# Three PSUM banks in turn for the down products of the looped rounds

## What is computed

```python
def swiglu(h, w_gu, w_down):
    gt, up = jnp.split(h @ w_gu, 2, axis=-1)
    return (jax.nn.silu(gt) * up) @ w_down

def short_conv_mixer(h, w_in, w_conv, w_out):
    bg, cg, xv = jnp.split(h @ w_in, 3, axis=-1)
    return (bg * dwconv(cg * xv, w_conv, SC_PAD)) @ w_out

def reference(...):
    h, hc = x, ctx
    for l in range(DEPTH):                      # DEPTH = 2
        sh1, sc1, g1, sh2, sc2, g2 = adaln(c, mod_w[l], mod_b[l])
        n_lat = modulate(rmsnorm(h, norm1_g[l]), sh1, sc1)
        if l % 2 == 0:
            y, yc = hybrid_mixer(n_lat, n_ctx, ...)
        else:
            y = short_conv_mixer(n_lat, o_w_in[o], o_conv_w[o], o_w_out[o])
        h = h + g1 * y
        h = h + g2 * swiglu(modulate(rmsnorm(h, norm2_g[l]), sh2, sc2), ffn_w_gu[l], ffn_w_down[l])
    return rmsnorm(h, final_g)
```

## Time and profile before

| | |
|---|---|
| median of 3 runs | 2563.57 us (2562.7 to 2565.39) |
| the profiled execution | 2565.16 us, its span 2563.0 us |
| TensorE busy | 2459.5 us, 96% of the span |
| VectorE busy | 1128.1 us, 44% |
| TensorE waiting for sumsq (normalisations) | 27.8 us, 5 times |
| TensorE waiting for an update of h | 21.7 us, 37 times |
| mean granted clock of TensorE | 0.989 |

### The profile page before, as it was taken

How to read it: one execution, slowest core, us unless ns; L and a number is a source line. 1 busy time by engine, 2 the same in 40 slices (tenths; PEclk the granted TensorE clock), 3 DMA queues, 4 the chain that set the end, 5 groups by cost and what they waited for, 6 DMA issues and landing times.

```text
span 2563.0 us, 29648 instructions
## 1 busy us (share of the span) xinstructions
PE 2459.5 (96%) x11210; PEld 1996.6 (78%) x11210; DVE 1128.1 (44%) x1460; ACT 524.7 (20%) x805; POOL 1067.1 (42%) x511
## 2 busy tenths in 40 slices
PE   7899999989899999999999899999799999999999
PEld 3677877768788888888888688887688888888887
DVE  4666648755843444422223634245622222222224
ACT  3344437751200000000001200002200000000003
POOL 2143336899533444333444234342533333333440
PEclk9999999999999999999999899999899999999999
DMA  9543366433233332311111011111111111111111
GB/s 284 149 134 128 128 174 135 89 97 107 91 115 115 112 100 91 105 50 49 49 49 50 17 50 50 41 50 40 50 50 42 48 49 41 49 49 49 49 33 66
DMA packets 223198, 206.55 MB, mean 81 GB/s; under 512 B 40119, under 2 KB 193427, under 8 KB 222611
## 3 DMA queue, kind: packets, MB, share of 16 engines
q1 hardware_dynamic: 216643, 186.64, 25.1%
q10 hardware_dynamic: 5904, 16.78, 1.7%
q0 software_dynamic: 576, 2.10, 0.2%
HBM read 185.20 MB, written 20.28 MB: 80 GB/s over the span
## 4 chain that ended last, share of the span: by engine, by line
PE 85%; DVE 6%; POOL 3%; issue 3%; ACT 2%; DMA 1%; DVEq 0%; POOLq 0%; SPq 0%; ACTq 0%
PE bank L727 27%; PE bank L729 26%; PE bank L728 26%; DVE h L1365 1%; PE bank L850 1%; DVE probs L1568 1%; DVE sumsq L1321 1%; PE bank L808 1%; POOL k_lo L628 1%; PE bank L759 1%; PE bank L893 1%; DVE act_lo L1348 1%; DMA mod_ring<-in_mod_w 1%; DVE hid_f L1608 1%; ACT probs L1213 1%
## 5 line engine op out<-in xcount | busy, mean ns | idle before, releaser
L574 POOL TENSOR_TENSOR w_hi<-raw,ones 128x1024 fp32r<-128x1024 f32 x200 | 392.3, 1961 | 1240.0 <-PE bank L729 1191.6
L727 PE MATMUL bank<-act_hi,w_hi 128*128 128x512 f32 x2176 | 855.5, 393 | 13.4 <-DVE act_lo L1348 4.5
L728 PE MATMUL bank<-act_hi,w_lo 128*128 128x512 f32 x2176 | 851.7, 391 | 0.0
L729 PE MATMUL bank<-act_lo,w_hi 128*128 128x512 f32 x2176 | 851.6, 391 | 0.0
L577 POOL TENSOR_TENSOR w_lo<-raw,w_hi 128x1024 fp32r<-128x1024 f32 x200 | 509.9, 2550 | 15.7
L727 PEld LDWEIGHTS bank<-act_hi,w_hi 128*128 128x128 f32 x2176 | 411.3, 189 | 103.6 <-issue 7.6
L729 PEld LDWEIGHTS bank<-act_lo,w_hi 128*128 128x128 f32 x2176 | 411.1, 189 | 86.1
L728 PEld LDWEIGHTS bank<-act_hi,w_lo 128*128 128x128 f32 x2176 | 411.5, 189 | 84.5
L1365 DVE SCALAR_TENSOR_TENSOR h<-bank,mods,h 128x512 f32<-128x512 f32 x432 | 320.6, 748 | 244.5 <-PE bank L729 242.4
L1608 DVE TENSOR_TENSOR hid_f<-silu_g,bank 128x512 f32<-128x512 f32 x88 | 60.6, 689 | 706.9 <-PE bank L729 705.6
L727 PE MATMUL bank<-hid_hi,w_hi 128*128 128x512 f32 x704 | 281.2, 399 | 15.8 <-DVE h L1365 15.8
(11 more groups left out here) (187 smaller groups left out, 2329.8 us busy)
## 6 DMA issues: line engine op xcount, KB each, us to landing
raw<-in_ffn_w_gu SPq DMA_DIRECT2D x88, 512.0 KB, 3.9
mod_in_f<-in_mod_w SPq DMA_DIRECT2D x48, 512.0 KB, 4.7
raw<-in_ffn_w_down SPq DMA_DIRECT2D x44, 512.0 KB, 3.6
mod_in_p<-in_mod_w SPq DMA_DIRECT2D x32, 512.0 KB, 6.7
raw<-in_o_w_in SPq DMA_DIRECT2D x24, 512.0 KB, 3.7
raw<-in_e_w_in SPq DMA_DIRECT2D x20, 512.0 KB, 4.9
mod_ring<-in_mod_w SPq DMA_DIRECT2D x16, 512.0 KB, 5.0
raw<-in_e_w_out SPq DMA_DIRECT2D x16, 512.0 KB, 3.9
```

The costliest lines, as they stand in the source:

```text
L574: nc.gpsimd.tensor_tensor(w_hi, raw[:, parity, :], ones[:, 0:1].to_broadcast([P, UNIT]), ALU.mult).then_inc(s_hi, 1)
L727: pe.matmul(dst, w_hi, x_hi, start=first, stop=False)
L728: pe.matmul(dst, w_lo, x_hi, start=False, stop=False)
L729: return pe.matmul(dst, w_hi, x_lo, start=False, stop=last)
```

## The change

`out_groups` and `update` get a number of banks, `turn`: 3 where the round does not feed a normalisation, 2 where it does. Group idx writes bank 4 + idx % turn, so banks 4, 5 and 6 in the looped rounds. Groups below `turn` have no wait any more, but group 0, which waits until all updates of the rounds before are done; group idx from `turn` on waits for update idx - turn.

```diff
+                turn = 3 if norm is None else 2
                 for idx in range(16):
                     half, m = divmod(idx, FT)
-                    pe.wait_ge(s_hup, n0 + idx + 1)
-                    group(half, m, bank[:, 4 + m % 2, :]).then_inc(s_out, 1)
+                    if idx == 0 or idx >= turn:
+                        pe.wait_ge(s_hup, n0 + max(idx - turn, 0) + (3 if idx else 2))
+                    group(half, m, bank[:, 4 + idx % turn, :]).then_inc(s_out, 1)
...
-            def update(n0, idx, gate):
+            def update(n0, idx, gate, turn=2):
...
-                V.scalar_tensor_tensor(out=dst, in0=bank[:, 4 + m % 2, :], scalar=mods[:, gate, m:m + 1], in1=dst,
+                V.scalar_tensor_tensor(out=dst, in0=bank[:, 4 + idx % turn, :], scalar=mods[:, gate, m:m + 1], in1=dst,
...
-                        update(16 * i + OUT_F[layer], idx, MODS * layer + G2)
+                        update(16 * i + OUT_F[layer], idx, MODS * layer + G2, 3)
...
-                    update(16 * i + OUT_F[0], idx, G2)
+                    update(16 * i + OUT_F[0], idx, G2, 3)
...
-                    update(16 * i + OUT_S, idx, MODS + G1)
+                    update(16 * i + OUT_S, idx, MODS + G1, 3)
```

## The result

| | before | after |
|---|---|---|
| median, 4 runs each | 2564.48 us (2562.7 to 2567.2) | 2540.02 us (2538.85 to 2541.62) |
| the profiled execution | 2565.16 us, span 2563.0 | 2539.45 us, span 2537.3 |
| TensorE busy | 2459.5 us, 96% | 2451.8 us, 97% |

What follows compares the result with a forecast made beforehand. TensorE's matmuls plus its holes were taken to bound the kernel. Savings of 10.9 + 10.4 + 2.1 = 23.4 us made 2540.2 us against a median of 2563.57, range 2535 to 2547.

Steps and rivals of the forecast that it cites:

- The sum: All looped rounds: 10.9 plain, 10.4 modulation and 2.1 short-convolution save 23.4 us, giving 2540.2 us.
- The bound: TensorE's matmuls and holes set the time; 29 of 37 waits for h, 13.3 us, lie in looped rounds.
- The plain rounds: Rounds 6 to 9 of layer 0, 0 to 9 of layer 1: group 2's hole goes, 14 x 0.78 = 10.9 us.
- The slack of group 3: Plain rounds, three banks: update 0 is over 0.7 us before group 3 would start.
- The modulation rounds: Six rounds adding a modulation row: holes at groups 2, 4, 7, 10 go, 6 x (1.86 - 0.12) = 10.4 us.
- The term for group 5: Modulation rounds: with 0.13 us of slack behind update 2, group 5 costs 0 to 0.25 us; half was charged.
- The short-convolution rounds: Three looped short-convolution rounds lose a hole of 0.71 us each, 2.1 us.
- The clock: Behind the normalisations the 1.2 GHz level may fall on other matmuls: 3 us either way.
- The wait did not move on to group 5: Rival, modulation rounds: group 5 waits 0.58 us as group 4 did, 2543.0 us; chance 0.05.
- The spacing inside the products: Rival, down products: the new bank order slows steps from 0.227 to 0.233 us, 2551.7 us; chance 0.03.
- something else holds group 2: Rival: something the trace hides behind this wait holds group 2 as long, so no gain, 2563.6 us; chance 0.03.
- The slower rival: TensorE drops to 1.2 GHz, one 1.4 us piece in each of 23 changed rounds, 2572 us; chance 0.02.

Runs made afterwards that it cites:

- the copies: A 128 x 256 VectorE copy added ahead of update 0 in the 14 plain rounds of the changed kernel: within SBUF 2566.92 us, from bank 7 2538.93 us.
- the pair of copies: A 128 x 256 copy out of bank 7 ahead of update 0 in plain rounds: kernel before, two banks, 2569.23 us; changed kernel, three banks, 2538.93 us.
- the run with the SBUF copy and two banks: Kernel before plus a 128 x 256 copy within SBUF ahead of update 0 in the 14 plain rounds: 2615.15 us, ratio 1.0205.
- the last rounds: Changed kernel plus a third bank in the last feed-forward round of layer 0 and the last short-convolution round: 2541.41 us, ratio 0.9911.
- a moved instruction: Kernel before, update 0 moved ahead of the last hid_lo or z_lo: all looped rounds 2557.88 us; 14 plain rounds alone 2565.73 us (2557.27 to 2582.29).

## Why the prediction was right

**The number.** The sum was 23.4 us and the medians say 24.5; the periods say 24.7. That 2540.2 and 2540.02 lie 0.2 us apart is in part luck: the sum was 1.1 us short, and the median of the kernel before, with a fourth run, is 0.9 us higher than the one the forecast started from. The 0.6 us that the clock gave back in the passages is luck too.

**The bound.** That the holes of TensorE are the time, and that 29 of the 37 lie in the changed rounds, held: 28 fewer waits are shown after, 9 against 37, and none is left in the looped rounds. (The one too many is in the last round of layer 0, where the 1.2 GHz level now falls on other matmuls of the same work.)

**The plain rounds.** Forecast 65.4, measured 65.33. The cost of a hole, read from starts and not from the idle column, was right: 0.51 us is shown as idle, 0.78 was counted and 0.80 came. The other 0.02 us may be the steps of 0.24 and 0.23 that follow the restart; the rows resolve no more. The slack of group 3, worked out as 0.7 us, is shown by the copies: 0.34 us is hidden, and of 2.35 us all but 0.65 comes through.

**The modulation rounds.** Forecast 67.4, measured 67.26. The term for group 5 was mis-sized: half of 0.25 us was charged, and the cost is one step of 0.28 in place of 0.23. That is 0.07 of the 0.16 us by which the saving of 1.74 fell short of 1.90. The rest is hundredths in the steps behind the four restarts, as in the plain rounds, which the sum left out. TensorE in round 1 of layer 0, the start of group 5:

```profile
788.25 0.39 PE L729 MATMUL bank<-hid_lo,w_hi 128*128 128x512 f32 x1
788.47 0.43 PE L727 MATMUL bank<-hid_hi,w_hi 128*128 128x512 f32 x1
788.75 0.39 PE L728 MATMUL bank<-hid_hi,w_lo 128*128 128x512 f32 x1
```

VectorE at the same place:

```profile
785.59 2.10 DVE L1378 SCALAR_TENSOR_TENSOR mod_acc_f<-mod_in_f,cond,mod_acc_f 128x1024 f32<-128x1024 f32 x1
787.62 2.06 DVE L1367 SCALAR_TENSOR_TENSOR h<-bank,mods,h 128x512 f32<-128x512 f32 x3
```

The long mod_acc_f step is there as in the earlier trace rows, update 2 ends at about 787.62 + 0.75 = 788.37, and group 5 starts at 788.47. The slack was worked out as 0.13 us and is 0.10: enough. The charge was taken over from group 7 of the kernel before, but there update 5 ended at about 794.13 + 0.75 = 794.88, 0.09 us behind the natural start of 794.79 and not ahead of it. A release that much late cost 0.25 us; one that much early costs 0.05.

**The short-convolution rounds.** Forecast 0.71, measured 0.71.

**The clock.** The 1.2 GHz level fell on other matmuls behind the last round of layer 0 and behind the short convolution, as was held possible: 1.0 us won and 0.4 us lost, where 3 us either way were allowed for.

**The rivals.** The wait did not move on to group 5. The spacing inside the products is 0.227 with the bank order of the change. That something else holds group 2 is excluded by the changed kernel, where it starts without a hole, and by the pair of copies. The rule of the Trainium skill that spoke for no effect ("TensorE: Matmul & The Clock Gate", section "HAM oscillation") comes from a section on a kernel that waited for DMA. Here the holes were waits for a bank: the third one gave 24 us, and the fourth, with no wait for h left to remove, gave nothing. The slower rival, the drop to 1.2 GHz, did not occur in the changed rounds. But the run with the SBUF copy and two banks shows that it is real. TensorE behind its hole of 2.86 us in a round of layer 0:

```profile
1338.11 0.50 PE L727 MATMUL bank<-hid_hi,w_hi 128*128 128x512 f32 x1 [2.86 <-DVE h L1365]
1338.45 0.40 PE L728 MATMUL bank<-hid_hi,w_lo 128*128 128x512 f32 x1
```

And in a round of layer 1:

```profile
1869.57 0.80 PE L727 MATMUL bank<-hid_hi,w_hi 128*128 128x512 f32 x1 [2.86 <-DVE h L1365]
1870.16 0.63 PE L728 MATMUL bank<-hid_hi,w_lo 128*128 128x512 f32 x1
1870.59 0.63 PE L729 MATMUL bank<-hid_lo,w_hi 128*128 128x512 f32 x1
```

The hole is the same. In the second the steps are 0.43 us. Its round, by the start of the last hid_f of two rounds, takes 69.81 us, against 68.49 for a round without such a piece:

```profile
1864.02 0.69 DVE L1608 TENSOR_TENSOR hid_f<-silu_g,bank 128x512 f32<-128x512 f32 x1 [8.39 <-PE bank L729]
...
1933.83 0.69 DVE L1608 TENSOR_TENSOR hid_f<-silu_g,bank 128x512 f32<-128x512 f32 x1 [8.39 <-PE bank L729]
```

Eleven of the 14 plain rounds of this run have such a piece, and they take 69.8 to 70.1 us: 1.3 to 1.6 us for one piece, around the 1.4 us at which the earlier trace rows put it. Why three rounds escaped is not shown. A hole of 0.51 us never did this in the plain rounds of the kernel before.

## What to carry to other kernels

A wait for a buffer on the bounding engine is worth its whole length only where the engine that frees the buffer is not itself the bound: look at what the waiting engine would wait for next, as the last rounds show. Count a hole by the steps from start to start, since the restart costs too (0.80 us where 0.51 us was shown as idle), and work out the slack of the next groups with the same rows. Of two ways to the same gain, a third bank and a moved instruction, the one that leaves every engine's timing alone is the safer; the moved one met another engine to within 0.03 us, and whether it won or lost changed from round to round and from run to run.

## What the runs showed of the hardware

A VectorE instruction that reads two tensors in SBUF, or copies within SBUF, and that finds one of GpSimd's splits running, ends only behind it: the copy of 0.28 us took 2.43, hid_lo and z_lo of 0.69 us took 2.90 and 2.88. If VectorE is clearly first, GpSimd is the one that is held. VectorE and GpSimd in round 3 of layer 0 of the kernel before:

```profile
916.64 1.28 DVE L1376 SCALAR_TENSOR_TENSOR mod_acc_f<-mod_in_f,cond,mod_acc_f 128x1024 f32<-128x1024 f32 x1 [2.67 <-DMA mod_in_f<-in_mod_w]
```

```profile
916.97 2.71 POOL L574 TENSOR_TENSOR w_hi<-raw,ones 128x1024 fp32r<-128x1024 f32 x1 [0.74 <-PE bank L729]
```

w_hi, 1.89 us long elsewhere, begins 0.33 us behind the mod_acc_f step and takes 2.71. The update of h and the copy out of bank 7, which have at most one tensor to read in SBUF, are not held up: 0.75 and 0.41 us beside a running w_lo.

This also explains two lengths that the prediction took as given: hid_lo of 1.11 us, which stood beside w_hi, and the mod_acc_f step of 2.09 us beside w_lo; where GpSimd is idle they are 0.69 and 1.28. By these rows 0.42 us of the lateness of update 0 in a plain round came from GpSimd. That is an estimate: no run here took GpSimd's step away from that place.

The Trainium skill states this in "SBUF — State Buffer", section "Who interferes with whom": VectorE with two SBUF inputs, against a GpSimd instruction that reads SBUF, or VectorE in a mode that uses two ports, needs a pair of ports that the two engines share; the one that issues first has it for its whole instruction, and the other blocks. The rows with a clear order agree with it. The pairs that begin 0.03 us apart cannot tell: GpSimd's record is the first in both, and once it is GpSimd that is held.
